# The second block's norms: products on the centred input, with the inverse deviation multiplied in behind them

## What is computed

```python
def layer_norm(x, g, b):
    mu = jnp.mean(xf, -1, keepdims=True)
    var = jnp.mean(jnp.square(xf - mu), -1, keepdims=True)
    y = (xf - mu) * lax.rsqrt(var + LN_EPS) * g.astype(jnp.float32) + b.astype(jnp.float32)
...
    h = layer_norm(jnp.concatenate([meta, x], axis=1), emb_ln_g, emb_ln_b)
    for i in range(DEPTH):
        u = h @ w_in[i]
...
        mix = (jax.nn.sigmoid(u[..., GLU_END:GA_END]) * y_attn
               + jax.nn.sigmoid(u[..., GA_END:GC_END]) * y_conv) @ w_out[i]
        h = layer_norm(ALPHA * h + mix, ln1_g[i], ln1_b[i])
        if i % 2 == 0:
            f = swiglu(h, ffn_w_gate[j], ffn_w_up[j], ffn_w_down[j])
        else:
            f = moe_swiglu(h, router[j], moe_w_gate[j], moe_w_up[j], moe_w_down[j])
        h = layer_norm(ALPHA * h + f, ln2_g[i], ln2_b[i])
```

## Time and profile before

| | |
|---|---|
| median of 3 runs | 1981.0 us (1977.43 to 1989.36) |
| the profiled execution's time | 1982.48 us |
| its span, first to last instruction | 1980.7 us |
| mean granted TensorE clock | 0.939 of full |
| busy: PE, DVE, ACT, POOL | 1840.4, 1179.8, 1019.5, 990.5 us |
| HBM | 171 GB/s over the span |

### The profile page before, as it was taken

How to read it: one execution, slowest core, us unless ns; L and a number is a source line. 1 busy time by engine, 2 the same in 40 slices (tenths; PEclk the granted TensorE clock), 3 DMA queues, 4 the chain that set the end, 5 groups by cost and what they waited for, 6 DMA issues and landing times.

```text
span 1980.7 us, 31409 instructions
## 1 busy us (share of the span) xinstructions
PE 1840.4 (93%) x12590; PEld 1700.1 (86%) x12590; DVE 1179.8 (60%) x1693; ACT 1019.5 (51%) x1534; POOL 990.5 (50%) x597
## 2 busy tenths in 40 slices
PE   6999999998899998989989999989889999999996
PEld 5988899987789998968889999878878878888875
DVE  4655554454545534866644433777646887777883
ACT  3455554344545533656434432566435767676672
POOL 5431565542146653656225444467314767776660
PEclk8999999988989998999989999889878999999996
DMA  6522345542224554322225555322325888788880
GB/s 243 195 94 86 131 172 190 190 173 83 86 107 168 184 182 161 131 96 90 105 73 189 173 186 181 113 106 87 110 83 212 319 297 312 291 312 300 320 313 23
DMA packets 50024, 340.02 MB, mean 172 GB/s; under 512 B 5511, under 2 KB 7775, under 8 KB 10031
## 3 DMA queue, kind: packets, MB, share of 16 engines
q1 hardware_dynamic: 47152, 328.79, 45.8%
q0 software_dynamic: 2720, 9.13, 1.5%
HBM read 336.76 MB, written 1.13 MB: 171 GB/s over the span
## 4 chain that ended last, share of the span: by engine, by line
PE 74%; DVE 11%; ACT 6%; issue 5%; POOL 3%; DMA 0%; SPq 0%; DVEq 0%; ACTq 0%; POOLq 0%
PE bank L385 13%; PE bank L387 12%; PE bank L386 12%; PE bank L753 4%; PE bank L754 4%; PE bank L755 4%; ACT wh L941 3%; DVE CA L1592 3%; PE bank L411 2%; DVE wl L1358 2%; PE bank L463 2%; PE bank L521 2%; POOL wl L1907 2%; PE bank L523 2%; PE bank L522 2%
## 5 line engine op out<-in xcount | busy, mean ns | idle before, releaser
L1907 POOL TENSOR_TENSOR wl<-stg,wh 128x512 fp32r<-128x512 f32 x311 | 773.1, 2491 | 805.9 <-ACT wh L941 805.2
L1358 DVE TENSOR_TENSOR wl<-stg,wh 128x1536 fp32r<-128x1536 f32 x311 | 602.4, 1944 | 366.7 <-ACT wh L941 366.0
L941 ACT ACTIVATE wh<-stg 128x2048 fp32r<-128x2048 f32 x311 | 594.4, 1912 | 299.0 <-PE bank L387 170.1
L385 PE MATMUL bank<-xh,wh 128*128 128x256 f32 (+1 forms) x1568 | 462.1, 295 | 11.9 <-DVE xl L1542 6.7
L387 PE MATMUL bank<-xh,wl 128*128 128x256 f32 (+1 forms) x1568 | 453.2, 289 | 0.0
L386 PE MATMUL bank<-xl,wh 128*128 128x256 f32 (+1 forms) x1568 | 452.9, 289 | 0.0
L385 PEld LDWEIGHTS bank<-xh,wh 128*128 128x128 f32 x1568 | 301.9, 193 | 16.7 <-issue 13.1
L386 PEld LDWEIGHTS bank<-xl,wh 128*128 128x128 f32 x1568 | 302.2, 193 | 0.6
L387 PEld LDWEIGHTS bank<-xh,wl 128*128 128x128 f32 x1568 | 302.6, 193 | 0.0
L521 PE MATMUL bank<-wh,xh 128*128 128x256 f32 x480 | 145.7, 304 | 34.1 <-DVE xl L1397 17.4
L753 PE MATMUL bank<-wh,GH 128*128 128x512 f32 (+3 forms) x400 | 149.4, 373 | 0.7 <-DVE wl L1358 0.6
(11 more groups left out here) (226 smaller groups left out, 3238.3 us busy)
## 6 DMA issues: line engine op xcount, KB each, us to landing
stg<-in_w SPq DMA_DIRECT2D x311, 1024.0 KB, 4.8
BT<-bias_scratch POOLq DMA_DIRECT2D x3, 1024.0 KB, 11.4
BT<-bias_scratch POOLq DMA_DIRECT2D x1, 2048.0 KB, 12.2
BB<-bias_scratch POOLq DMA_DIRECT2D x2, 1024.0 KB, 8.0
res<-in_x SPq DMA_DIRECT2D x1, 1024.0 KB, 5.7
BB<-bias_scratch POOLq DMA_DIRECT2D x2, 512.0 KB, 8.9
...
```

Source lines behind the costliest of these rows:

```text
L385: pe.matmul(out, wh, xh(kt), start=kt == 0, stop=False)
L941: act.activation(WH[u % NW][:, :], stg[u % NS][:, :], ACT.Copy).then_inc(*m.inc("w_high", u))
L1358: vec.tensor_tensor(WL[u % NW][:, 0:VW], stg[u % NS][:, 0:VW], WH[u % NW][:, 0:VW].bitcast(F32), ALU.subtract).then_inc(*m.inc("w_low_v", u))
L1907: pool.tensor_tensor(WL[u % NW][:, VW:], stg[u % NS][:, VW:], WH[u % NW][:, VW:].bitcast(F32), ALU.subtract).then_inc(*m.inc("w_low_g", u))
```

## The change

For `mean_e`, `n10` and `n2` the input is only centred and multiplied by the gain before the products; since the deviation is one number a token, it is multiplied in behind them, and the bias, which it must not touch, goes through the products as one more column of the input (XH and XL are 274 wide, the last column zero). DVE centres straight from the bank of sums (`centred_split`). ACT writes XH and the square. POOL adds up the eight squares (`add_squares`), one product by ones gives the variance in all partitions (`variance`, behind product tile 2), and DVE makes the inverse deviation on 272 columns (`late_rstd`). The first two product tiles run feature tile by feature tile together (`gemm_pair`). Tiles 0 to 2 are evacuated after tile 2: DVE takes the bias column to `bw` and the multiplied tile to `ub`, and ACT does from there, with `bw` as the bias, what it did from the bank. The normalised RES is made on the side, a feature tile behind each of the product tiles 3 to 10 (`late_y`, `y_with_bias`). `dense` does the same with DBW, dt and du. `taps_due` starts a channel one tile later and catches up.

```diff
-        if nt >= 2 * c + 1:
+        if nt >= 2 * c + 2:
...
-        XH = sb("xh", [P, KD, T], F32R)
-        XL = sb("xl", [P, KD, T], F32R)
+        XH = sb("xh", [P, KD, T + 2], F32R)
+        XL = sb("xl", [P, KD, T + 2], F32R)
...
+            def gemm_pair(xh, xl, n, name, give_back, operand):
+
+                u, bs = at[0] // UT, [bank((name, nt), *give_back(nt)) for nt in range(2)]
+                unit_ready(u)
+                for kt in range(KD):
+                    operand(kt)
+                    for nt in range(2):
+                        b, old = bs[nt]
+                        out, k = PS[b][:, 0:n], slice((nt * KD + kt) * P, (nt * KD + kt + 1) * P)
+                        if kt == 0:
+                            vacant(old)
+                        pe.matmul(out, WH[u % NW][:, k], xh(kt), start=kt == 0, stop=False)
+                        pe.matmul(out, WH[u % NW][:, k], xl(kt), start=False, stop=False)
+                        ins = pe.matmul(out, WL[u % NW][:, k], xh(kt), start=False, stop=kt == KD - 1)
+                        if kt == KD - 1:
+                            ins.then_inc(*m.inc("group", (name, nt)))
+                m.also("group", ("unit", u))
+                at[0] += UT
+
...
-                    sums[name], old = bank((name, "mean"), ("mean", name))
+                    sums[name], old = bank((name, "mean"), ("centred", (name, KD - 1)) if name in late else ("mean", name))
...
+            def variance(name):
+                b, old = bank((name, "var"), ("var_out", name))
+                vacant(old)
+                w.wait_ge(*m.of("sq_added", (name, KD - 1)))
+                pe.matmul(PS[b][:, 0:T], ones, SQ[:, 0, 0:T], start=True, stop=True).then_inc(*m.inc("group", (name, "var")))
...
+                    if nt == 2:
+                        variance(st)
...
-                gemm(KD, 14, lambda kt: XH[:, kt, :], lambda kt: XL[:, kt, :], T, f"u{l}", give_back, halves_ready(st), pump)
-                gemm(KD, 16, lambda kt: XH[:, kt, lo:T], lambda kt: XL[:, kt, lo:T], n, f"g{l}", lambda nt: [("u_out", (l, nt + 14))],
-                     lambda kt: None, lambda nt: pump(nt + 14))
+                    return [("scaled_u", (l, nt))]
+
+                def operand_u(kt):
+                    w.wait_ge(*m.of("bias_col_low", st))
+                    halves_ready(st)(kt)
+
+                gemm_pair(lambda kt: XH[:, kt, :], lambda kt: XL[:, kt, :], T + 2, f"u{l}", give_back, operand_u)
+                gemm(KD, 14, lambda kt: XH[:, kt, :], lambda kt: XL[:, kt, :], T + 2, f"u{l}", give_back, None, pump, 2)
+                gemm(KD, 16, lambda kt: XH[:, kt, lo:T + 2], lambda kt: XL[:, kt, lo:T + 2], n + 2, f"g{l}",
...
-                layer_norm(f"o{l}", f"n1{l}")
+                if l == 0:
+                    late_sums("o0", "n10")
+                else:
+                    layer_norm("o1", "n11")
...
+                gemm_pair(lambda kt: XH[:, kt, :], lambda kt: XL[:, kt, :], T + 2, "gu", give_back, operand_gu)
+                gemm(KD, 44, lambda kt: XH[:, kt, :], lambda kt: XL[:, kt, :], T + 2, "gu", give_back, None,
+                     lambda nt: variance("n10") if nt == 2 else None, 2)
 
...
+            def centred_split(name, gname, bname, l, free):
+                w.wait_ge(*m.of("group", free))
+                w.wait_ge(*m.of("zero_col"))
+                act.activation(XH[:, :, T], small(bname, l * KD, KD), ACT.Copy).then_inc(*m.inc("bias_col_high", name))
                 for kt in range(KD):
-                    w.wait_ge(*m.of("normed_y", (name, kt)))
-                    act.activation(XH[:, kt, :], SQ[:, kt, :], ACT.Identity, bias=small(bname, l * KD + kt)).then_inc(*m.inc("x_high", (name, kt)))
-                for kt in range(KD):
-                    act.activation(RES[:, kt, :], SQ[:, kt, :], ACT.Identity, bias=small(bname, l * KD + kt)).then_inc(*m.inc("y_out", (name, kt)))
+                    w.wait_ge(*m.of("centred", (name, kt)))
+                    act.activation(XH[:, kt, 0:T], XC[:, kt, :], ACT.Copy, scale=small(gname, l * KD + kt)).then_inc(*m.inc("x_high", (name, kt)))
+                    act.activation(SQ[:, kt, :], XC[:, kt, :], ACT.Square).then_inc(*m.inc("centred_sq", (name, kt)))
+
+            def y_with_bias(name, bname, l, kt):
...
+                def with_bias(nt):
+                    ub, bw = a["ub"][nt % 4], a["bw"][:, nt:nt + 1]
+                    w.wait_ge(*m.of("scaled_u", (l, nt)))
+                    if nt < 8 and nt % 2 == 0:
+                        act.activation(a["HC"][:, nt // 2, 30:30 + T], ub[:, :], ACT.Tanh, scale=0.5, bias=bw).then_inc(*m.inc("u_out", (l, nt)))
...
+                def evac(nt):
+                    if nt < 2:
+                        return
+                    for n in range(0 if nt == 2 else nt, nt + 1):
+                        with_bias(n)
+                    if 3 <= nt < 3 + KD:
+                        y_with_bias(before, bname, 0, nt - 3)
...
+            def centred_split(name, gname, bname, l):
                 def low(kt):
                     w.wait_ge(*m.of("x_high", (name, kt)))
-                    vec.scalar_tensor_tensor(XL[:, kt, :], SQ[:, kt, :], small(bname, l * KD + kt), XH[:, kt, :].bitcast(F32), ALU.add,
+                    vec.scalar_tensor_tensor(XL[:, kt, 0:T], XC[:, kt, :], small(gname, l * KD + kt), XH[:, kt, 0:T].bitcast(F32), ALU.mult,
                                              ALU.subtract).then_inc(*m.inc("x_low", (name, kt)))
 
+                w.wait_ge(*m.of("bias_col_high", name))
+                vec.tensor_tensor(XL[:, :, T], small(bname, l * KD, KD), XH[:, :, T].bitcast(F32), ALU.subtract).then_inc(*m.inc("bias_col_low", name))
                 w.wait_ge(*m.last("res"))
-                centre(name, RES, KD)
-                deviation(name, KD)
-                spread(name)
-                scale_y(name, gname, l, KD, low)
+                w.wait_ge(*m.of("group", (name, "mean")))
+                for kt in range(KD + 1):
+                    if kt < KD:
+                        ins = vec.scalar_tensor_tensor(XC[:, kt, :], bank((name, "mean"))[:, 0:T], -1.0 / D, RES[:, kt, 0:T], ALU.mult, ALU.add)
+                        ins.then_inc(*m.inc("centred", (name, kt)))
+                    if kt > 0:
+                        low(kt - 1)
+
+            def late_rstd(name):
+                v, tmp = late[name][:, 0, :], late[name][:, 1, :]
+                w.wait_ge(*m.of("group", (name, "var")))
+                vec.tensor_scalar(v, bank((name, "var"))[:, 0:T], 1.0 / D, LN_EPS, ALU.mult, ALU.add).then_inc(*m.inc("var_out", name))
+                w.wait_ge(*m.last("var_out"))
+                rsqrt(v, BC[:, :], tmp, "rstd", name)
+                w.wait_ge(*m.last("rstd"))
+
+            def late_y(name, gname, l, kt):
+                w.wait_ge(*m.of("x_low", (name, kt)))
+                vec.scalar_tensor_tensor(XC[:, kt, :], XC[:, kt, :], small(gname, l * KD + kt), BC[:, :], ALU.mult,
+                                         ALU.mult).then_inc(*m.inc("normed_y", (name, kt)))
...
+                def scaled(nt):
+                    key, n0 = ((f"u{l}", nt), 0) if nt < 14 else ((f"g{l}", nt - 14), lo)
+                    ps, ub = bank(key), a["ub"][nt % 4]
+                    half = 1.0 if nt < 8 and nt % 2 or nt in (12, 13) else SCALE if 8 <= nt < 12 else 0.5
+                    w.wait_ge(*m.of("group", key))
+                    if nt >= 4:
+                        w.wait_ge(*m.of("u_out", (l, nt - 4)))
+                    vec.tensor_scalar(a["bw"][:, nt:nt + 1], ps[:, T - n0:T - n0 + 1], half, None, ALU.mult).then_inc(*m.step("v_step"))
+                    vec.tensor_tensor(ub[:, n0:T], ps[:, 0:T - n0], BC[:, n0:T], ALU.mult).then_inc(*m.inc("scaled_u", (l, nt)))
+
...
+                def gated(c):
+                    w.wait_ge(*m.of("u_out", (l, 2 * c + 1)))
+                    w.wait_ge(*m.of("pad_zero", l))
+                    vec.scalar_tensor_tensor(HC[:, c, 30:30 + T], HC[:, c, 30:30 + T], 1.0, a["ub"][(2 * c + 1) % 4][:, :], ALU.add,
+                                             ALU.mult).then_inc(*m.inc("gated", (l, c)))
...
+                    if nt < 2:
+                        return
+                    if nt == 2:
+                        late_rstd(before)
+                    for n in range(0 if nt == 2 else nt, nt + 1):
+                        scaled(n)
+                    if nt in (2, 4, 6, 8):
+                        gated(nt // 2 - 1)
+                    if 3 <= nt < 3 + KD:
+                        late_y(before, gname, 0, nt - 3)
...
-                    if not up:
+                    k, ps = nt % 3, bank(("gu", i))
+                    w.wait_ge(*m.of("group", ("gu", i)))
+                    if up and nt >= 3:
+                        w.wait_ge(*m.of("h_high", ("d", nt - 3)))
+                    if not up and nt >= 3:
+                        w.wait_ge(*m.of("hidden", nt - 3))
```

(39 more changed lines are left out.)

121 lines of the change are left out of this document (64 added, 57 removed).

## The result

The changed kernel takes **1994.2 us** in the median (1989.7 to 1998.3, 15 runs), against 1980.2 for the kernel before, timed beside it (15 runs). The ratio is 1.0069, 95% interval 1.0057 to 1.0082: 14 us slower, inside 1%. The profiled execution spans 1992.2 us.

A forecast was written before the change was run, and what follows sets the result against it. PE was taken to bound the dense stage, DVE largely both mix layers. +10 for each mix layer and 9 won in the dense stage sum to +11 on the profiled 1982.5: 1992 us on the median, range 1962 to 2008.

The forecast's parts named there:

- 16.5 us won per norm at its start: From the mean's end to two finished product tiles, each norm would take 8.4 us instead of 24.9.
- A pause of 1.6 should not cost the clock: PE's pause of about 1.6 us behind each norm's mean would leave its clock full.
- The pair of evacuation and multiply, 0.43: DVE's one-column evacuation and multiply, per product tile, would cost 0.43 us back to back.
- Rival (c): Each DVE pair costs its full 0.58 us, slowing mix layers and dense loop: 2004 us; chance 25%.
- `late_rstd` 7 us: DVE's 12 dependent passes over 272 columns for the inverse deviation would take 7 us, 6 to 8 in all.
- Mix layers +10 each: Each mix layer, running largely at DVE's pace, would get 10 us longer, with ends of +2 and +16.
- DVE over 90% busy: Sign to look for: DVE over 90% busy in the mix layer's first fourteen product tiles.
- Rival (b): Mix layers come out even as POOL's contention thins, and the dense stage gives 10 to 14: about 1968 us; chance 18%.
- Dense stage, 9 us won: The shorter norm less the stage's added costs would win 9 us in the dense stage, 5 to 14.
- `low` 0.41, which stood in ACT's shadow: In the dense loop, DVE's previously hidden pass would add 0.41 us, within a loop of 5.87, just under PE's 6.1.
- Two more columns in 2496 matmuls: 2.3 us in all: PE's matmuls over two more columns would cost 2.3 us in all, 1.0 of it in the dense stage.
- (a): PE counts everywhere and DVE's additions hide, so 46 us come off: 1935 us; chance 12%.

The follow-up runs named there:

- rows_274: The kernel before with only the rows of XH and XL declared 274 columns long instead of 272, accesses unchanged; 1985.3 us, ratio 1.0035.
- wide_rows: The kernel before, old scheme everywhere, with XH and XL rows of 274 columns and two zero fills of the added columns; 1987.1 us, ratio 1.0043.
- early_split: The changed kernel with ACT's split of the next weight unit ahead of its evacuation of odd product tiles, not behind; 1963.1 us, ratio 0.9916.
- low_back: The changed kernel with the dense stage's subtraction L1786 put behind the next odd product tile's evacuation, not the next even one's; 1988.4 us, ratio 1.0037.
- early_low_280: The changed kernel with ACT's split before odd-tile evacuations, L1786 behind the next odd tile's evacuation, and XH and XL rows 280 long; 1951.7 us, ratio 0.9869.

## Why the prediction was right, and where it was not

The time (1992 against 1994.2), the side and the range hold. The sum holds by luck in good part: two of its terms were twice or more too large, of opposite signs, and a third was missing. Measured, the mix layers cost 9.8 where +20 stood, the dense stage gave 2.0 where 9 stood, and the rows cost about 7 beyond the 2.3 us put down for their two more columns.

1. **16.5 us won per norm at its start.** The pauses came as told, 1.90 and 1.79 against 1.6. The eight feature tiles came a little slower: by PE's timeline the pair is done 9.0 us behind the mean's end in the second and third norm (1015.66 to 1024.62, 1235.41 to 1244.40), 8.4 forecast, and 9.6 in the first, where the clock fell. The old norm took 24.4 (1009.7 to 1034.12), not 24.9. So 15.0 to 15.5 were won, not 16.5. "A pause of 1.6 should not cost the clock" failed in one norm of three, at a price of about 0.6. Since the kernel before was at half its clock there as well (778 to 795), and a pause of 1.79 left it full, the pause's length alone doesn't tell when it falls.
2. **The pair of evacuation and multiply, 0.43.** Right: median 430 ns for the multiply, the next instruction 0.34 on (795.29 to 795.63), and 0.42 from pair to pair. Rival (c), which hung on 0.55 or more, is out, though its time would have been 2004.
3. **`late_rstd` 7 us.** It took 6.0 (789.2 to 795.2), within 6 to 8. Most passes took 0.44; the shift 0.92 was not foreseen and paid for by the others.
4. **Mix layers +10 each.** They cost 4.8 and 5.0, and 0.4 to 2.4 of that is the rows' (`rows_274`: 170.8 and 159.7; `wide_rows`: 170.2 and 161.1), so the term was two to three times too large. The mechanism named first, DVE as the pace, was wrong for the first fourteen tiles: "DVE over 90% busy" met 16.64 of 22.30. The step that failed is the taps. I kept them at the contended 1.0 us, but in the changed kernel they took 498 ns in the median (1002 before) and 674 in the mean (987), 37 us less for 120 of them. That is more than the 60 multiplies and their small copies cost (26 us at 0.43), and so DVE had room. Rival (b) had half of this, in that POOL's contention would thin. That fewer of them meet POOL's passes is what the durations look like; why they do is not shown, and it isn't DVE's wait for ACT alone, since `early_split` has no such waits and a median of 500. The second part is the wait for ACT: I wrote 1.0 a period and it was 0.9 to 2.6, in the mean about 1.8. `early_split` shows what it costs: 12 and 10 us in the mix layers. The prediction's own terms for the five periods (4.3 for the pairs, 2.9 for `late_y`, 5.0 of waits on 35.7) add up to 47.9, not to its 45.4; measured from split to split it was 42.8 (801.39 to 844.18). The split of tile 14 came 0.4 later than before, counted from the mean, where I said 3.8. From mean to last DVE tap it took 169.7 us, not 177.
5. **Dense stage, 9 us won.** 2 us were won, and only 0.7 against `wide_rows`. From the first dense product to the next norm's it took 219.8, and about 215 was forecast. The step that failed is above all one term, "`low` 0.41, which stood in ACT's shadow": L1786 took 1.12 behind POOL's split and stood ahead of the multiply that ACT waits for. It made the loop 6.46 in place of 5.87, over PE's pace, times some 17 periods. Of the rest 1 to 1.5 us is the gain at the norm's start, which was smaller than 16.5 (item 1), and about as much the periods with `late_y`, 7.36 and not 7.0. `low_back`, in which the pass takes 0.43 and stands behind that multiply, wins 7.3 against before in this stretch, near the forecast's 9.
6. **Missing: the rows.** "Two more columns in 2496 matmuls: 2.3 us in all" counts only the work. The new declaration made PE's other matmuls about 1% slower from the first block on: 7 us, shown by `rows_274`.
7. **Rivals.** (a), PE counts everywhere, would be 1935. Even with all three side costs taken away the kernel is at 1952, since the first tiles of the mix layers then run at DVE's pace (`early_split`: 21.13 of 22.30 busy). The busiest engine by the page was PE both times; by the window no engine was full in the changed kernel's mix layer. (b) is out as well: no mix layer came out even, though its thinner contention did come about (item 4).

What stays open: why rows of 1096 B cost. PE's matmuls are slower even where they read HH and HL, not XH, and the unused tile of 128 B moved those as far as `rows_274` did. In `rows_274` and `early_low_280` both the row's length and the place of XL differ from before; the one was not told from the other. Also open are 1.5 us in each of the last two stretches of the changed kernel, and the 5 to 8 us between kernels of one program behind `n11`.
